# Expert layers: vector work before and after the token gates dealt out anew, gate products and output updates moved ahead of their waits

## What is computed

```
s = einsum('bthcd,hcnd->bthcn', (x @ w_q).reshape(...), sub_keys)   # 8 heads, 2 sides, 128 keys
top_s, top_i = top_k(s, 16);  best_s, pos = top_k(top_s row + col, 16)
idx = row * 128 + col;        gate = softmax(best_s)                # 128 picks a token
h = gelu(x . exp_u[idx]);     out = sum_k gate_k * h_k * exp_v[idx_k]
x = layer_norm(DN_ALPHA * x + out)
```

## Time and profile before

| | us |
|---|---|
| median of 3 runs | 2561.87 |
| lowest, highest | 2560.5, 2565.36 |
| the profiled execution | 2559.97 |
| its span, first to last instruction | 2558.2 |
| mean granted TensorE clock | 0.986 of 2.4 GHz |

### The profile page before, as it was taken

One profiled execution on the slowest core, in us unless ns is written; L12 is line 12 of the kernel. 1 busy time (PEld: TensorE's weight loads), 2 busy tenths in 40 slices (PEclk: granted clock), 3 DMA queues, 4 the chain that ended last, 5 costly groups with the idle time before them and its releaser, 6 DMA issues. The chain is left out here.

```text
span 2558.2 us, 61258 instructions
## 1 busy us (share of the span) xinstructions
PE 2418.5 (95%) x22900; PEld 2273.8 (89%) x22900; DVE 1635.7 (64%) x3403; ACT 1310.9 (51%) x2406; POOL 596.7 (23%) x494
## 2 busy tenths in 40 slices
PE   5998899999989999999999999889999999999998
PEld 3998567578978999999999998769999999999997
DVE  3032632635445967777888666756967777887665
ACT  3322643357345665555445554455665555445554
POOL 0335133157336930000000000637920000000000
PEclk9999999999999999999999999989999999999999
DMA  8554023044113554444444554324554444444552
GB/s 275 179 162 138 17 74 96 22 122 132 45 60 133 188 188 166 164 164 164 165 164 164 190 188 161 119 76 146 184 191 155 164 164 165 165 164 166 191 184 83
DMA packets 153875, 373.31 MB, mean 146 GB/s; under 512 B 8920, under 2 KB 102888, under 8 KB 137232
## 3 DMA queue, kind: packets, MB, share of 16 engines
q1 hardware_dynamic: 151232, 369.27, 42.8%
q10 hardware_dynamic: 2512, 2.24, 0.3%
HBM read 370.44 MB, written 1.05 MB: 145 GB/s over the span
## 5 line engine op out<-in xcount | busy, mean ns | idle before, releaser
L3015 ACT ACTIVATE w_hi<-ring 128x512 fp32r<-128x512 f32 x1024 | 641.7, 632 | 684.0 <-PE bank L3070 362.5
L3021 DVE TENSOR_TENSOR w_lo<-ring,w_hi 128x512 fp32r<-128x512 f32 x864 | 588.9, 689 | 345.4 <-ACT w_hi L3015 340.4
L3052 PE MATMUL bank<-x_hi,w_hi 128*128 128x256 f32 x2048 | 575.9, 281 | 7.0 <-DVE w_lo L3021 6.8
L3070 PE MATMUL bank<-hidden_hi,w_hi 128*128 128x256 f32 x2048 | 574.9, 281 | 0.0
L3070 PE MATMUL bank<-hidden_hi,w_lo 128*128 128x256 f32 x2048 | 573.2, 280 | 0.0
L3052 PE MATMUL bank<-x_hi,w_lo 128*128 128x256 f32 x2048 | 572.8, 280 | 0.0
L3052 PE MATMUL bank<-x_lo,w_hi 128*128 128x256 f32 x2048 | 571.4, 279 | 0.0
L3070 PE MATMUL bank<-hidden_lo,w_hi 128*128 128x256 f32 x2048 | 570.2, 278 | 0.0
L375 POOL TENSOR_TENSOR w_lo<-ring,w_hi 128x512 fp32r<-128x512 f32 (+3 forms) x260 | 337.6, 1317 | 649.5 <-ACT w_hi L366 641.5
L3052 PEld LDWEIGHTS bank<-x_hi,w_hi 128*128 128x128 f32 x2048 | 385.7, 188 | 8.0 <-issue 7.2
L3052 PEld LDWEIGHTS bank<-x_lo,w_hi 128*128 128x128 f32 x2048 | 385.7, 188 | 0.0
(11 more groups left out here) (522 smaller groups left out, 3977.1 us busy)
## 6 DMA issues: line engine op xcount, KB each, us to landing
ring<-in_peer_uT SPq DMA_DIRECT2D x128, 1024.0 KB, 4.9
ring<-in_peer_v SPq DMA_DIRECT2D x128, 1024.0 KB, 4.8
ring<-in_even_w_in SPq DMA_DIRECT2D x26, 1024.0 KB, 5.4
ring<-in_ada_w SPq DMA_DIRECT2D x24, 1024.0 KB, 7.8
ring<-in_odd_w_in SPq DMA_DIRECT2D x12, 1024.0 KB, 5.3
ring<-in_even_w_out SPq DMA_DIRECT2D x8, 1024.0 KB, 5.9
ring<-in_odd_w_out SPq DMA_DIRECT2D x8, 1024.0 KB, 5.2
ring<-in_peer_w_q SPq DMA_DIRECT2D x8, 1024.0 KB, 5.2
```

The lines of the kernel that those rows point to most:

```text
L3015: act.activation(k.hi[q][:, :], k.ring[slot][:, q * PART:q * PART + PART], ACT.Copy).then_inc(k.hi_ready, 1)
L3021: eng.tensor_tensor(k.lo[q][:, :], k.ring[slot][:, q * PART:q * PART + PART], k.hi[q][:, :].bitcast(F32), ALU.subtract).then_inc(k.lo_read ...
L3052: mm = pe.matmul(k.bank[s][:, j * T:j * T + T], a[q][:, w], b[:, cc, :], start=(cc == 0 and n == 0), stop=(cc == KC - 1 and n == 2))
L3070: mm = pe.matmul(out, a[q][:, w], b[:, j, :], start=first and cc % 2 == 0 and n == 0, stop=last and cc % 2 == 1 and n == 2, skip_group_che ...
```

## The change

In round 7 `turn_picks` follows column 0. DVE copies the indices behind the lows of column 2 and splits the gates in two steps, behind columns 3 and 4; the onehots of the first two groups go behind columns 5 and 7. At the end of the up phase the onehots of phase 1's first two groups take the two places in the last block that stood empty, and PE does these groups' gates ahead of its wait for the gelus. At the end of down the first two of the four additions wait for one part less. The instructions themselves are the same ones.

```diff
--- before.py
+++ after.py
@@ -3102,7 +3102,7 @@
                 self.up_column(pe, r, n // PAIR, n % PAIR)
         for n in range(STEPS):
             self.up_column(pe, ROUNDS - 1, n // PAIR, n % PAIR)
-            if n == PAIR - 1:
+            if n == 0:
                 self.turn_picks(pe)
         with pe.Fori(0, ROUNDS) as r:
             for n in range(STEPS):
@@ -3112,11 +3112,12 @@
                 self.up_column(pe, r + ROUNDS, n // PAIR, n % PAIR)
 
 
-        pe.wait_ge(self.stored, ROUND + STREAM)
         for n in range(STEPS):
             if n % BLOCK == 0:
                 self.dense_gates(pe, 2 * ROUNDS, n // 2)
                 self.dense_gates(pe, 2 * ROUNDS, n // 2 + 1)
+            if n == 0:
+                pe.wait_ge(self.stored, ROUND + STREAM)
             self.down_column(pe, 2 * ROUNDS, n // PAIR, n % PAIR, first=n == 0)
         with pe.Fori(1, ROUNDS) as r:
             for n in range(STEPS):
@@ -3263,21 +3264,27 @@
         S.settle(dve)
         dve.tensor_tensor(gate, gate, spread(self.sums, 3, 16), ALU.mult).then_inc(self.picked, 1)
 
-    def split_gates(self, dve):
+    def split_indices(self, dve):
 
         k, S = self.k, self.k.dve
         dve.wait_ge(self.turned, 1)
         S.step(dve.tensor_copy(self.rowT[:, :, :], spread(k.bank[6][:, 0:T], 2, 2)))
         S.step(dve.tensor_copy(self.colT[:, :, :], spread(k.bank[6][:, T:2 * T], 2, 2)))
+
+    def split_gates(self, dve, part):
+
+        k, S = self.k, self.k.dve
         gates = spread(k.bank[7][:, 0:T], 2, 2)
-        S.step(dve.tensor_copy(self.gateT[:, :, 0, :], gates))
         S.settle(dve)
-        S.step(dve.tensor_tensor(self.rest, gates, self.gateT[:, :, 0, :], ALU.subtract))
-        S.settle(dve)
-        S.step(dve.tensor_copy(self.gateT[:, :, 1, :], self.rest))
-        S.settle(dve)
-        S.step(dve.tensor_tensor(self.gateT[:, :, 2, :], self.rest, self.gateT[:, :, 1, :], ALU.subtract))
-        S.settle(dve)
+        if part == 0:
+            S.step(dve.tensor_copy(self.gateT[:, :, 0, :], gates))
+            S.settle(dve)
+            S.step(dve.tensor_tensor(self.rest, gates, self.gateT[:, :, 0, :], ALU.subtract))
+        else:
+            S.step(dve.tensor_copy(self.gateT[:, :, 1, :], self.rest))
+            S.settle(dve)
+            S.step(dve.tensor_tensor(self.gateT[:, :, 2, :], self.rest, self.gateT[:, :, 1, :], ALU.subtract))
+            S.settle(dve)
 
     def onehots(self, dve, phase, r, n):
 
@@ -3328,6 +3335,8 @@
         self.apply(dve, phase, r, m)
         if not last:
             self.onehots(dve, phase, r, m + 2)
+        elif phase == 0:
+            self.onehots(dve, 1, 0, 0)
         self.low_block(dve, lows, n + 2)
         if phase:
             self.hidden_low(dve, r, n + 2)
@@ -3337,6 +3346,8 @@
             self.hidden_low(dve, r, n + 3)
         if not last:
             self.onehots(dve, phase, r, m + 3)
+        elif phase == 0:
+            self.onehots(dve, 1, 0, 1)
         self.low_block(dve, lows, n + 4)
         if phase:
             self.hidden_low(dve, r, n + 4)
@@ -3355,9 +3366,13 @@
                 self.normalise(dve)
         for n in range(STEPS):
             self.low_block(dve, ROUNDS - 1, n)
-            if n == PAIR + 1:
-                self.split_gates(dve)
+            if n == 2:
+                self.split_indices(dve)
+            if n in (3, 4):
+                self.split_gates(dve, n - 3)
+            if n == 5:
                 self.onehots(dve, 0, 0, 0)
+            if n == 7:
                 self.onehots(dve, 0, 0, 1)
         self.low_block(dve, ROUNDS, 0)
 
@@ -3366,8 +3381,6 @@
                 self.gate_block(dve, 0, r, n)
         for n in range(0, STEPS, BLOCK):
             self.gate_block(dve, 0, ROUNDS - 1, n, n == STEPS - BLOCK)
-        self.onehots(dve, 1, 0, 0)
-        self.onehots(dve, 1, 0, 1)
         self.hidden_low(dve, 0, 0)
         with dve.Fori(0, ROUNDS - 1) as r:
             for n in range(0, STEPS, BLOCK):
@@ -3388,9 +3401,9 @@
             at = slice(2 * q, 2 * q + 2)
             k.dve.step(dve.tensor_tensor(y[:, at, :], k.xh[:, at, :].bitcast(F32), k.xl[:, at, :].bitcast(F32), ALU.add))
         k.dve.settle(dve)
-        dve.wait_ge(k.consumed, self.h0 + 4 * ROUNDS * ROUND * PARTS)
         for q in range(KC // 2):
             at = slice(2 * q, 2 * q + 2)
+            dve.wait_ge(k.consumed, self.h0 + 4 * ROUNDS * ROUND * PARTS - (q < KC // 4))
             dve.scalar_tensor_tensor(out=y[:, at, :], in0=y[:, at, :], scalar=DN_ALPHA,
                                      in1=k.bank[q][:, :].rearrange("p (c t) -> p c t", c=2), op0=ALU.mult, op1=ALU.add).then_inc(self.updated, 1)
 
```

## The result

| | before | after |
|---|---|---|
| median of 6 runs each, us | 2564.07 (2560.5 to 2565.36) | 2549.74 (2544.47 to 2554.03) |
| profiled execution | 2559.97 | 2548.27 |
| its span | 2558.2 | 2546.5 |

The ratio is 0.9946, 95% interval 0.9934 to 0.9957, so 0.54% less (11.0 to 16.9 us). The forecast was 2549.2 and 12.7 us less; the medians differ by 14.3, the two profiled executions by 11.7. That the forecast time came within 0.5 us is in part luck: it was reckoned from a median of before of 2561.87 (3 runs), which with 6 runs is 2564.07.

The account below looks back on a forecast made before the run. PE bounds the expert layers, so only its few waits there can be given back. 3.64 + 4.98 + 2 x 1.0 + 2 x 1.05 = 12.7 us off the median 2561.87 gives 2549.2; range 2546 to 2556.

Parts of the forecast that it names:

- First edit: Round 7, both expert layers: dealing out DVE's work ends PE's stall; 3.64 us in the first, 4.98 in the second.
- the 1.6 left at two places: Round 7: the lows of parts 8 and 12, the tightest, end with 1.6 us left, so PE never waits.
- The general slack: Round 7: DVE may be 2.64 us late with a low before PE notices; no piece is longer.
- The clock: Round 7, second layer: the fall to 1.2 GHz behind the stall goes too; 1.29 us of the 4.98.
- the 1.29: Round 7, second layer: extra us from half clock behind the stall; by the free-running watch, luck of this execution.
- rival B: Second layer's clock fall was chance, or one comes elsewhere; gives back 1.3 to 2.6 us, 2551; chance 0.11.
- Second edit: Start of down: gates run ahead of the gelu wait with onehots already made; 1.0 us a layer.
- Third edit: End of down: earlier additions let PE go straight on to the products with ones; 1.05 us a layer.
- A: Round 7: onehots behind column 5 or 7 make PE wait 1 to 2 us a layer; 2552.2; chance 0.13.
- C: Round 7's stall only moves, to `turned` or the gates, leaving 4.1 us of gain; 2557.8; chance 0.05.
- D: Behind the first layer, the clock falls after waits where it now stays up; slower, 2574; chance 0.03.

Follow-up runs that it names:

- one_piece_early: The changed kernel with all of round 7's dealt-out DVE work in one piece behind column 2's lows, transposes as in the change; one time, 2561.12 us.
- experiments 6 and 7: 6: the kernel before with the first edit alone, median 2556.96 us, ratio 0.9966. 7: the changed kernel without its first edit, median 2558.62 us, ratio 0.9976.
- all_but_round7: The changed kernel without its first edit, so round 7 as before; median 2558.62 us of 8 runs, ratio 0.9976.

## Why the prediction was right

- **First edit.** Predicted 3.64 and 4.98, measured 3.68 and 4.97 in the profiled pair. That PE would not wait at all was right, and so were the 1.6 left at two places (1.5). The general slack was not: 2.64 counted only the time from a low's end to its use. Before its next low DVE also stands idle for 0.7, and that is free too; the limit for one piece is 3.3, by two kernels (3.35, 3.29). The error was on the safe side and changed no term. The limit is that of a piece with nothing but parts on PE beside it. Of the single pieces of 7.57 in the kernel before and 7.70 in one_piece_early, 4.0 and 3.7 were covered; there the transposes, 0.57 of PE's time, lie among the parts, which is probably the difference, though no run was made to show it.
- **The clock.** That the 1.29 was chance was right, as rival B had it; its size was not. The kernels with the 3.4 us stall give eight samples of it: cost 3.68 three times with no fall, and 4.97, 5.14, 6.10, 6.22 and 6.28 with one. The mean is 4.97, so 9.9 for two, where the sum had 8.6 and bounds of 1.3 either way for the whole. A stall with a fall behind it cost up to 2.6 more than the same stall without, where the prediction allowed at most one fall of 1.29 a layer. This term is the one that was mis-sized. It would account for the medians' 14.3 and 16.3 where 12.7 was forecast (9.9 + 1.9 + 2.0 to 2.4 is 14), but the times don't show that it does: the interval of the result, 11.0 to 16.9, holds 12.7 as well, and on the chip of experiments 6 and 7 the medians gave 6.4 for the first edit and 4.7 for the other two, 11.1 together.
- **Second edit.** 1.0 a layer, measured 0.95 and 0.98. The next wait was named rightly, the chain gelu, high, low; making the high early took all of it away. Both halves of the edit are needed (2.89 and 3.38 with one of them, 2.40 with both).
- **Third edit.** 1.05 a layer, measured 1.11 on PE, and 1.19 and 0.80 up to the layer norm, against an upper bound of 1.11. The 0.08 more is the products with ones, which took 3.69 behind the wait and 3.62 without. The 0.80 is smaller through the step between blocks, which no row of before had shown. That loss is not the third edit's: alone it gave 1.2 in both layers, and the first edit alone has the longer step. The sum had no term for it.
- **The rivals.** A: no new wait in any layer. C: no stall moved. D: no loss of clock elsewhere; the mean granted clock was 0.986 in both profiles, and 0.95 over 1590 to 1840 in both.

## What to carry to other kernels

Measure how long an engine may stay away from a feed that it shares (here three parts of cover and its own idle, 3.3 us), then cut every other job that it has into pieces below that, with enough feed between them to catch up. A stall of an engine whose clock can fall may cost more than its length, and by an amount that changed here from run to run: price it by the mean of several, not by one trace. Where two things are late at one point, moving one gives nothing (PE's wait alone) or a part (the onehots alone, half); move both, and then look at what is late third.

## What the runs showed that was not expected

**The dearness of a stall.** Behind waits of 0.2 and 1.4 to 1.5 us the clock stayed up, 4 of 4; behind 3.40 to 3.45 it fell to 1.2 GHz in 5 of 8, behind 3.8 in 2 of 2, and then 12 to 25 matmuls started 0.21 apart. The length alone did not decide it: a stall of 3.44 had no fall, one of 3.40 had one. The moment moved as well. In all_but_round7 the granted clock fell before PE went on (0.78 over 985 to 986, first matmul at 986.86), in one_piece_early's first layer 1 us after. By the Trainium skill, TensorE: Matmul & The Clock Gate, section Part 1, the moment of the change depends on where a free-running watch stands. The eight samples of nearly the same stall, which end in no fall, a short one or a long one, agree with it; that such a watch is the cause is not shown by them.

**Two steady paces.** With the clock at 1.00 and no wait in any record, PE runs a whole stretch of an expert layer at one of several paces. In the second half of down (1536 matmuls) it is 0.1167 or 0.1178 us a matmul, and so 381.7 or 383.4 us for the whole of down in most profiles. Equal stretches of 170 us in that half, which hold no other matmuls, in the kernel before, second layer and first (length, PE busy and count, clock, DMA share, GB/s):

```profile
2360.00:2530.00 170.00, 170.00 (x1446) 1.00 0.49 173
1410.00:1580.00 170.00, 170.00 (x1459) 1.00 0.52 182
```

and in the kernel after, likewise:

```profile
2350.00:2520.00 170.00, 170.00 (x1459) 1.00 0.48 173
1410.00:1580.00 170.00, 170.00 (x1446) 1.00 0.53 182
```

13 matmuls fewer in the same time, before in the second layer and after in the first. The slow pace stood in 14 of 26 such stretches in the 13 profiles, in the first layer, the second, both or none, and differently in two profiles of the same changed kernel. So it is not a matter of the code alone. The longer spacing is not at the parts' edges: it recurs in every three matmuls, whose starts lie 0.119, 0.116 and 0.118 apart at the slow pace and 0.117, 0.117 and 0.116 at the fast one, and no gap between two starts in these halves is over 0.120. What sets it stays open. At 1.7 us a stretch it is part of the distance between runs of one kernel, which is up to 10 us.

**The step between blocks.** In the second layer, the 0.4 more between the products with ones and the layer norm appeared in all seven profiles in which round 7 had no stall of over 0.3 us, and in none of the six that had one. So the first edit, which takes the stall away, seems to give back 0.4 there. No run was made to tell why.
